# Gated linear attention taken from the middle chunk outwards, context pairs two places later, and the gate row loaded first

## The reference, cut to what matters

```python
def step(S, inp):                      # GLA, one direction, one chunk
    qc, kc, vc, gc = inp
    b = jnp.cumsum(gc, axis=1)
    ...
    scores = jnp.einsum('bihk,bijhk,bjhk->bhij', qc, decay, kc)
    o_intra = jnp.einsum('bhij,bjhv->bihv', scores, vc)
    o_inter = jnp.einsum('bihk,bhkv->bihv', qc * jnp.exp(b), S)
    k_dec = kc * jnp.exp(b[:, -1:] - b)
    S_new = jnp.exp(b[:, -1])[..., None] * S + jnp.einsum('bjhk,bjhv->bhkv', k_dec, vc)
    return S_new, o_intra + o_inter
...
u = ca * jax.nn.sigmoid(cb)            # convolution module
u = (_dwconv_grid(u, conv_dw_w) if latent else _dwconv_seq(u, conv_dw_w)) + conv_dw_b
...
x = x + gate1 * m                      # m: the mixer's output projection
...
act = jax.nn.gelu(jnp.einsum('td,thkd->thk', xb, u_tab[ib]))   # PEER
return jnp.einsum('thk,thkd->td', gb * act, v_tab[ib])
```

## Time and profile before

| | us |
|---|---|
| three runs | 3768.62, 3770.41, 3768.61 |
| median of the runs | 3768.62 |
| the profiled execution | 3767.62 |
| its span, first to last instruction | 3765.4 |
| busy: PE, DVE, POOL, ACT | 3234.2, 2710.0, 1388.9, 949.5 |
| mean granted TensorE clock | 0.932 |

### The profile page before, as it was taken

One profiled execution on the slowest core, in us unless ns is written; L12 is line 12 of the kernel. 1 busy time (PEld: TensorE's weight loads), 2 busy tenths in 40 slices (PEclk: granted clock), 3 DMA queues, 4 the chain that ended last, 5 costly groups with the idle time before them and its releaser, 6 DMA issues.

```text
span 3765.4 us, 35688 instructions
## 1 busy us (share of the span) xinstructions
PE 3234.2 (86%) x10985; PEld 1639.6 (44%) x10985; DVE 2710.0 (72%) x6429; ACT 949.5 (25%) x2553; POOL 1388.9 (37%) x1235
## 2 busy tenths in 40 slices
PE   7688989865689998567778699999999999999998
PEld 4355333322434444234434344444444444444444
DVE  2637698568534545788898589788788888776676
ACT  1322322462512112255735501110011111111011
POOL 1000567457544445333233233333333333333331
PEclk9889989966889999798998899999999999999999
DMA  9153878779788898999999999999999999999996
GB/s 354 71 176 123 307 258 267 261 263 341 268 290 294 295 348 302 381 373 355 332 399 386 368 367 402 382 416 406 391 407 413 409 408 405 416 406 397 397 410 272
DMA packets 308332, 1272.13 MB, mean 338 GB/s; under 512 B 30240, under 2 KB 82976, under 8 KB 221872
## 3 DMA queue, kind: packets, MB, share of 16 engines
q0 software_dynamic: 170448, 962.31, 66.4%
q1 hardware_dynamic: 135104, 301.91, 21.7%
q10 hardware_dynamic: 2592, 5.64, 0.4%
HBM read 1220.16 MB, written 49.58 MB: 337 GB/s over the span
## 4 chain that ended last, share of the span: by engine, by line
PE 30%; issue 23%; DVE 20%; DMA 17%; POOL 7%; ACT 3%; SPq 0%; POOLq 0%; DVEq 0%; ACTq 0%
DMA arena<-in_uv,idx 7%; PE bank L1108 6%; DMA ring_e<-in_uv,idx 5%; PE bank L916 4%; PE bank L1078 4%; PE bank L944 4%; DVE arena L1948 3%; POOL arena L805 3%; DVE ring_e L1948 2%; PE wide L859 2%; POOL ring_e L805 2%; PE wide L1129 2%; DVE arena L1979 2%; DVE arena L2006 1%; DMA ring_e<-in_v_rows,idx 1%
## 5 line engine op out<-in xcount | busy, mean ns | idle before, releaser
L805 POOL DMA_INDIRECT arena<-in_uv,idx x384 | 450.9, 1174 | 834.4 <-PE bank L1141 521.9
L1196 PE MATMUL bank<-arena 128*128 128x384 f32 x2048 | 693.8, 493 | 59.6 <-ACT arena L1629 36.6
L1948 DVE CUSTOM_DVE_ANT_0 arena<-arena,h2e 128x1024 f32<-128x1024 f32 x384 | 460.5, 1221 | 152.0 <-DMA arena<-in_uv,idx 150.8
L1196 PEld LDWEIGHTS bank<-arena 128*128 128x128 f32 x2048 | 390.8, 192 | 374.0 <-issue 137.5
L805 POOL DMA_INDIRECT ring_e<-in_uv,idx x256 | 302.2, 1180 | 633.4 <-PE bank L1141 349.9
L761 POOL DMA_INDIRECT ring_e<-in_u_rows,idx x256 | 317.2, 1239 | 497.0 <-DVE dots_e L1872 332.8
L1209 PE MATMUL wide<-arena 128*128 128x512 f32 x1024 | 462.4, 594 | 6.9 <-DVE arena L2018 6.9
L1544 ACT ACTIVATE small<-small 128x4 f32<-128x4 f32 x160 | 32.7, 204 | 1432.6 <-DVE small L1948 1432.6
L1948 DVE CUSTOM_DVE_ANT_0 ring_e<-ring_e,h2e 128x1024 f32<-128x1024 f32 x256 | 307.0, 1220 | 94.5 <-DMA ring_e<-in_uv,idx 94.2
L1872 DVE CUSTOM_DVE_ANT_0 ring_e<-ring_e,h2e 128x1024 f32<-128x1024 f32 x256 | 304.2, 1220 | 66.7 <-DMA ring_e<-in_u_rows,idx 64.9
L770 POOL DMA_INDIRECT ring_e<-in_v_rows,idx x256 | 280.9, 1097 | 125.7 <-issue 67.7
(11 more groups left out here) (276 smaller groups left out, 4375.0 us busy)
## 6 DMA issues: line engine op xcount, KB each, us to landing
arena<-in_ut SPq DMA_DIRECT2D x128, 512.0 KB, 7.9
arena<-in_uv SPq DMA_DIRECT2D x128, 512.0 KB, 8.2
arena<-in_w_q SPq DMA_DIRECT2D x48, 512.0 KB, 7.5
spread_d<-arena SPq DMA_DIRECT2D x12, 2048.0 KB, 24.5
arena<-spread_d SPq DMA_DIRECT2D x96, 256.0 KB, 10.7
ring_e<-in_w_mod POOLq DMA_DIRECT2D x16, 1024.0 KB, 8.9
arena<-in_w_cols SPq DMA_DIRECT2D x24, 512.0 KB, 6.2
arena<-in_x SPq DMA_DIRECT2D x20, 512.0 KB, 5.4
```

Of the source, the lines that this page charges most:

```text
L805: pool.indirect_dma_start(out=ring[r], out_offset=None, in_=a["uv"], in_offset=bass.IndirectOffsetOnAxis(ap=idx[kept(t)][:, k:k + 1], axis ...
L1196: ins = pe.matmul(s_bank[:, 0:NC], lhsT=utb[i % URING][:, k * P:(k + 1) * P], rhs=H2T[1][:, k, P:P + NC], start=(k == 0), stop=(k == KD - 1))
L1948: dve.tensor_tensor_reduce(out=ring[r][:, 0:D], in0=ring[r][:, 0:D], in1=h2b[kept(t)], scale=1.0, scalar=0.0, op0=ALU.mult, op1=ALU.add, a ...
```

## The change

Three things, on all engines at once.

1. *Pairs.* The phase conv has 14 places instead of 16, and each call in it carries an index lower by two: the first pair comes two projections later. All pairs up to attn stand two places later. The last phase, qf1, gets 17 pairs on its 16 places instead of 15; the last of the places has two.
2. *GLA.* The phases states and attn become one, gla, with 24 places. The chunks are attended in the order 3, 4, 2, 5, 1, 6, 0, 7, and an attend place p stands behind the state step that completes what it needs: place 0 in step 3, places 1 and 2 in step 4, 3 and 4 in step 5, 5 and 6 in step 6, 7 to 9 in step 7. An output waits for the states of its own step, where before there was one wait for all states. ACT's pair of a place stands at the place's end; before, pair c-1 stood behind the scb drains of chunk c. For the context stream the order is step 0, place 0, step 1, places 1 to 3.
3. *SP.* The gate row is loaded first, with a semaphore of its own (`gate1_in`), then x, then the rows shift2 and a2. DVE waits for these two only at the second norm.

The helpers and the table:

```diff
+GLA_STEPS = STREAMS[1][1] - STREAMS[1][0]
+def middle_out(n):
+    return sorted(range(n), key=lambda c: (max(c, n - 1 - c), c))
+def attend_at(n, i):
+    order = middle_out(n)
+    after = [max(order[0], n - 1 - order[0]) - 1] + [max(c, n - 1 - c) for c in order] + [n - 1]
+    return [p for p, step in enumerate(after) if step == i]
...
-        for phase, sites, pairs in (("conv", 16, 16), ("qk", 9, 9), ("vg", 16, 16), ("ln", 8, 8), ("gates", 8, 8), ("states", 14, 14),
-                                ("attn", 10, 10), ("out", 16, 16), ("qf0", 16, 16), ("qf1", 16, 15)):
+        for phase, sites, pairs in (("conv", 14, 14), ("qk", 9, 9), ("vg", 16, 16), ("ln", 8, 8), ("gates", 8, 8),
+                                    ("gla", 24, 24), ("out", 16, 16), ("qf0", 16, 16), ("qf1", 16, 17)):
...
+        gla_places = [(i, what) for i in range(GLA_STEPS) for what in
+                      [("state", i, j) for j in range(2) if i < GLA_STEPS - 1] + [("attend", p) for p in attend_at(GLA_STEPS, i)]]
+        gla_place = {what: n for n, (i, what) in enumerate(gla_places)}
```

SP:

```diff
+                sp.wait_ge(*S["mod_out"].at(2))
+                sp.wait_ge(*S["bank_full"].at(("o", t1 - 1)))
+                sp.dma_start(gate1b, mod_d[s, 2 * D:3 * D].partition_broadcast(P)).then_inc(*S["gate1_in"].mark(s, 16))
                 for t in range(t0, t1):
-                    sp.wait_ge(*S["bank_full"].at(("o", t1 - 1)))
                     sp.dma_start(X1[:, t - t0, :], a["x"][t * P:(t + 1) * P, :]).then_inc(*S["x1_in"].mark(s, 16))
-
-                sp.wait_ge(*S["mod_out"].at(2))
-                for dst, row in ((gate1b, 2), (shift2b, 3), (a2b, 4)):
+                for dst, row in ((shift2b, 3), (a2b, 4)):
```

PE; the calls of early on ACT and DVE change alike:

```diff
                         project("cb", m, *blk)
-                        early(s, "conv", 4 * m + 2 * j - 2)
+                        early(s, "conv", 4 * m + 2 * j - 4)
                         project("ca", m, *blk)
-                        early(s, "conv", 4 * m + 2 * j - 1)
+                        early(s, "conv", 4 * m + 2 * j - 3)
...
+                def out_chunk(p):
+                    c = order_[p]
                     t = t0 + c
+                    pe.wait_ge(*S["st_kept"].at((s, max(c, steps - 1 - c), 3)))
                     pe.wait_ge(*S["scT"].at(t))
...
+                for i in range(steps):
+                    if i < last:
+                        state_step(i)
+                    for p in attend_at(steps, i):
+                        if p < steps:
+                            score_chunk(p)
+                        if 1 <= p <= steps:
+                            out_chunk(p - 1)
+                        if p >= 2:
+                            turn_chunk(p - 2)
+                        early(s, "gla", gla_place[("attend", p)])
```

ACT:

```diff
-                    if c:
-                        early(s, "attn", c - 1)
-                    if 1 <= c <= steps:
-                        o_stats(c - 1)
-                    if c >= 2:
-                        turn_out(c - 2)
-                early(s, "attn", steps + 1)
+                        if 1 <= p <= steps:
+                            o_stats(p - 1)
+                        if p >= 2:
+                            turn_out(p - 2)
+                        early(s, "gla", gla_place[("attend", p)])
```

DVE, ahead of the output projection's drains:

```diff
-                dve.wait_ge(*S["bc_in"].at(s))
+                dve.wait_ge(*S["gate1_in"].at(s))
                 dve.wait_ge(*S["x1_in"].at(s))
```

139 lines of the change are left out of this document (72 added, 67 removed).

## The result

The changed kernel takes 3789.66 us (median of 5 runs, 3782.74 to 3794.02), the kernel before 3768.62 in the five runs that stood beside it (3761.76 to 3775.91). The ratio is 1.0052, 95% interval 1.0039 to 1.0065: slower by 0.5%, 15 to 25 us. Forecast were 3778 and a range of 3756 to 3788: the direction was right, the loss was forecast at less than half its size (9.2 us of 21.0), and the time lies 1.7 us above the range. The profiled execution of the changed kernel is its fastest, 3782.74.

The account below looks back on a forecast made before the run. Bound: PE in the convolution's projections, DVE from 484 to 575 us and in state steps, DMA in gathers, a ring of waits in the attend loop. Terms -10.9 - 0.7 + 19.8 - 1.5 + 1.0 + 1.5 = +9.2 gave 3778 us, range 3756 to 3788.

Parts of the forecast that it names:

- 1. Convolution: Convolution: pairs two projections later bring the decay projections from 574.22 to near 563.3, -10.9 us (bounds -4.2 and -14.8).
- The walk: Convolution's end: place-for-place working through PE's order, by which its waits there grow by some 5.6 us.
- 3. Latent GLA: Latent GLA: the same instructions in a new order cost +19.8 us in sum (bounds -7 and +21.5).
- 3a: Attend turns: ACT's pair ahead of the scb drains delays PE's out by some 3.15 us in seven turns, +22.2.
- (c): Last state step of the GLA: out(6) waits for the last kept products, made behind dots, +1.0 us.
- (b): GLA: three state steps between attend places need not wait for gathers, -2.5 us; first attend place gets state work behind it, -2.5.
- (d): Attend turns: two full-clock turns may drop to half clock, 1.68 us each, half taken: +1.6; 3.3 if nearly all outs do.
- 5. The pairs that come back in qf1: Last phase: one more pair beside PE's round, +1.0 us; four more transfers in the last place, +1.5 (0 to 6).
- mixing pays: GLA rival: state-step work fills DVE's waits in four turns, -7.0 us for the latent GLA, total 3751; chance 0.13.
- Hidden behind state steps: GLA rival: PE has matmuls during the drain wait in four turns; three pay, +9.6 not +22.2, total 3765; chance 0.22.
- The pick steps decide: Convolution's end, rival: DVE bounds, so only -4.2 us there, and all outs run at half clock; total 3786; chance 0.17.
- nothing moves: Whole kernel, rival: the same chain ends last everywhere, 3769 us; chance 0.03.

Follow-up runs that it names:

- part 1 alone: Only the pairs moved on the kernel before: two projections later in conv, 17 in qf1 instead of 15; ratio 1.0000 (0.9988 to 1.0012).
- ACT's order alone: On the kernel before, only ACT's attend-loop pair moved to the place's end, ahead of the next scb drains; 3797.34 against 3768.82 us, ratio 1.0079.

## Why the prediction missed, step by step

*1. Convolution.* Forecast -10.9, measured -11.9 in the changed kernel and -11.5 with the part alone. The walk held: no wait before the first pair, 20.9 us of waits at the end against some 21.5 as worked out (the 15.9 of all three waits before, 6.79, 6.10 and 3.03 at 488.05, and 5.6). The gain stays up to the state steps (287.9 behind it, 287.4 before).

*2. Context chunks.* Forecast -0.7, within 1 either way; measured +1.6, so this term had the wrong sign. The start of the latent stream varies by 8 us between the profiles and says nothing of it, but the stage itself does: from the first transposed keys of the context stream to the first block of its output projection PE takes 29.1 us before (179.41 to 208.51) and 30.7 in the changed kernel (181.53 to 212.24). In the seven profiles with the old order of chunks it takes 27.0 to 29.1, in the seven with the new one 30.7 to 31.2. Which wait it is was not followed.

*3. Latent GLA.* Forecast with the head of the output projection 19.8 - 1.5 = 18.3, measured 17.0 (15 to 23 in the other three kernels with this order). The mechanism of 3a is as written: outputs 3.95 us behind the normalise where 3.9 was worked out, waits of 3.1. On the old order of chunks it costs 25.3 with the clock, where the forecast had 22.2 and 1.6. In the changed order its size was wrong, and the sum came out by luck. The wait for the drain was counted in seven turns; three pay it in full and one 1.11 us of it, and putting ACT's order back gives 8 us, not 22. In its place each turn behind a state step pays something that was not in the forecast: its scores stand behind a pair that waits for v rows (2.78 and 2.02 us in the last two). The runs split the 17 us into 8 for ACT's order and 8 for that pair (209.0, 200.9, 192.5), each from one profile, where profiles of one order spread by 8 us; by the ratios it is 9 and 14 us, where each ratio has an interval of 4 to 5 us either way. Term (c), 1.0, is near what is seen where ACT's wait is there too (3.95 against 3.09); with ACT's order put back the 3.95 stand alone. The two terms of 2.5 in (b) no run separates. Nothing of (d) is seen: three of eight outputs run at the full clock in both kernels.

*4. Gate row.* Forecast about nothing for the row itself; the part alone is 0.9995 (0.9984 to 1.0006). The 1.5 for the head can't be told from the GLA.

*5. The pairs that come back in qf1.* **This is the step that failed.** Forecast +1.0 and +1.5; measured +16.0 in the queries and -0.9 behind them. "One more pair of 1.07 beside PE's round" was costed by PE's work alone. The pair's 2 MB lie at the one place of the phase that had been left free, while rows of x, the gate and the final norm are loaded and a query weight is due. The weight's wait is 9.42 and the half clock behind it 2.05, together 11.5 of the 16.0; one pair more (1.07) and small waits for v rows with slower blocks behind them (1259.05, 1388.91) are the rest. The kernel with part 1 alone has the same wait, and the one that leaves the first place free has none. The range reached 3788 because its slow end was built from parts 1 and 3 only, and the upper bound of 6 in this step was for the last place, not for the first. The measured lengths sum to -11.9 + 0.5 + 17.0 - 1.2 + 16.0 - 0.9 = +19.5, with the 1.6 of the context +21.1, for 21.0 between the medians; single stages are not known so well that this closeness means much.

The rivals: *mixing pays* fell in the kernel as changed. Put right on ACT and PE, the order reaches 192.5, not less than the old 192.0, so no gain of the mixing is seen even then; the wait of 3.95 us for the last kept products is still in it, and no run tried it without. The Trainium skill (Perfetto Trace Analysis, Optimization Strategy) says only that performance may improve by such interleaving; here the DMA share of the stretch fell from 0.88 to 0.79, so no run here shows that gain. *Hidden behind state steps* was right on the drain's wait and wrong on the sum: three turns pay it, as the rival said, and the 8 us that ACT's order is worth are near its 9.6 and far from the 22.2 of the forecast; but the scores behind a pair take the place of what is hidden. *The pick steps decide* fell with part 1 at -11.9, not -4.2; *nothing moves* fell with the 12.66 us.

On the clock, six outputs in a row ran at the half clock in the kernel with ACT's order alone, each behind waits of 2.55 and 3.09 us; behind the 2.55 alone both levels are seen. The Trainium skill's statement (TensorE: Matmul & The Clock Gate, Part 1) that the throttled state is the default and activity releases it fits the six. The clock's 5.1 us there are more than (d)'s 3.3. In the changed kernel, for which (d) was worked out, the outputs behind the state steps did not fall to the half clock as the prediction drew from that statement: the one at 999.17 ran at the full one, and as many did as before.

## What to carry to other kernels

In a loop that is a ring of waits, look where each in-order queue does work that the ring doesn't need, and keep it behind the drain that frees the next buffer: 1.3 us of gelu, weights and diag, and with them the wait for two dots, ahead of a drain cost 25 us on an engine that was a third idle. A place in a table of filler work that holds nothing may be what lets a weight load land in time; before filling it, read what the DMA queues carry there, and cost a filler by its bytes, not only by its matmuls. When an order is interleaved, check at each seam what now stands ahead of the first instruction of the next stage on every queue.
